# Latent attention with the values as the stationary operand, and softmax sums applied by channel

## What is computed

```python
q_nope, q_pe, k_nope, k_pe, v = ...      # per head: 64 + 32 query and key channels, 64 value channels
s = einsum('bqhd,bkhd->bhqk', q_nope, k_nope) + einsum('bqhr,bkr->bhqk', q_pe, k_pe)
p = softmax(s * scale, axis=-1)          # 256 queries, 512 keys (context and latent)
o = einsum('bhqk,bkhd->bqhd', p, v)
mix = o.reshape(b, 256, 1024) @ w_out
```

## Time and profile before

| | |
|---|---|
| median of three runs | 1434.42 us |
| the profiled execution, whole time | 1433.67 us |
| its span | 1431.8 us |
| TensorE busy | 1337.4 us (93%) |
| VectorE busy | 833.6 us (58%) |
| ScalarE busy | 558.0 us (39%) |
| mean granted clock | 0.976 |

### The profile page before, as it was taken

How to read it: one execution, slowest core, us unless ns; L and a number is a source line. 1 busy time by engine, 2 the same in 40 slices (tenths; PEclk the granted TensorE clock), 3 DMA queues, 4 the chain that set the end, 5 groups by cost and what they waited for, 6 DMA issues and landing times.

```text
span 1431.8 us, 16689 instructions
## 1 busy us (share of the span) xinstructions
PE 1337.4 (93%) x6768; PEld 1081.7 (76%) x6768; DVE 833.6 (58%) x1163; ACT 558.0 (39%) x739; POOL 3.5 (0%) x10
## 2 busy tenths in 40 slices
PE   5999879999899999999999999998789988799998
PEld 4877668888777778867777777887667766688887
DVE  5666666668664455563535352547556665667777
ACT  5354354455421122423131313125456553554542
POOL 0000000000000000000000000000000000000000
PEclk9999989999999999999999999999889998899999
DMA  8536365535554432454535353312021221235541
GB/s 306 196 118 250 121 275 211 196 130 206 198 180 181 198 118 88 164 218 147 206 141 212 136 217 137 140 51 92 30 83 48 96 81 60 110 137 207 193 176 59
DMA packets 23780, 218.75 MB, mean 153 GB/s; under 512 B 3104, under 2 KB 8224, under 8 KB 10656
## 3 DMA queue, kind: packets, MB, share of 16 engines
q1 hardware_dynamic: 21328, 209.67, 39.8%
q10 hardware_dynamic: 1520, 4.98, 0.9%
q0 software_dynamic: 864, 3.15, 0.6%
HBM read 216.74 MB, written 1.05 MB: 152 GB/s over the span
## 4 chain that ended last, share of the span: by engine, by line
PE 77%; DVE 12%; ACT 6%; issue 3%; DMA 1%; SPq 0%; DVEq 0%; ACTq 0%
PE bank L454 19%; PE bank L455 18%; PE bank L456 18%; PE bank L466 8%; PE bank L467 4%; DVE w_lo L1444 4%; PE mod_ps L503 3%; PE turned L482 3%; ACT w_hi L982 2%; DVE scaled L1485 2%; PE bank L867 2%; PE small L873 1%; DMA raw<-in_w_in 1%; DVE gated L1799 1%; PE small L522 1%
## 5 line engine op out<-in xcount | busy, mean ns | idle before, releaser
L1444 DVE TENSOR_TENSOR w_lo<-raw,w_hi 128x2048 fp32r<-128x2048 f32 (+4 forms) x168 | 338.2, 2054 | 80.4 <-ACT w_hi L982 79.8
L982 ACT ACTIVATE w_hi<-raw 128x2048 fp32r<-128x2048 f32 (+4 forms) x168 | 280.1, 1716 | 206.4 <-PE bank L456 169.6
L454 PE MATMUL bank<-act_parts,w_hi 128*128 128x512 f32 (+1 forms) x600 | 225.1, 375 | 1.8 <-DVE act_parts L1469 1.8
L466 PE MATMUL bank<-act_parts,w_hi 128*128 128x512 f32 x608 | 217.4, 402 | 6.6 <-DVE act_parts L1469 4.2
L455 PE MATMUL bank<-act_parts,w_hi 128*128 128x512 f32 (+1 forms) x600 | 221.8, 370 | 0.0
L456 PE MATMUL bank<-act_parts,w_lo 128*128 128x512 f32 (+1 forms) x600 | 221.6, 369 | 0.0
L467 PE MATMUL bank<-act_parts,w_lo 128*128 128x256 f32 x608 | 171.7, 282 | 0.0
L454 PE MATMUL bank<-w_hi,h_hi 128*128 128x512 f32 x392 | 154.5, 394 | 7.0 <-DVE h_lo L1721 3.6
L455 PE MATMUL bank<-w_lo,h_hi 128*128 128x512 f32 x392 | 152.8, 390 | 0.0
L456 PE MATMUL bank<-w_hi,h_lo 128*128 128x512 f32 x392 | 152.7, 389 | 0.0
L466 PEld LDWEIGHTS bank<-act_parts,w_hi 128*128 128x128 f32 x608 | 115.6, 190 | 35.3 <-DVE act_parts L1469 4.6
(11 more groups left out here) (234 smaller groups left out, 1636.9 us busy)
## 6 DMA issues: line engine op xcount, KB each, us to landing
raw<-in_ffn SPq DMA_DIRECT2D x35, 2048.0 KB, 7.7
raw<-in_mlp SPq DMA_DIRECT2D x24, 2048.0 KB, 7.6
raw<-in_mod_gate SPq DMA_DIRECT2D x7, 2048.0 KB, 7.7
raw<-in_conv_in SPq DMA_DIRECT2D x8, 1536.0 KB, 7.0
raw<-in_w_gates SPq DMA_DIRECT2D x4, 2048.0 KB, 8.3
raw<-in_w_branch SPq DMA_DIRECT2D x4, 2048.0 KB, 7.7
raw<-in_mla_q SPq DMA_DIRECT2D x4, 1152.0 KB, 5.1
raw<-in_w_in SPq DMA_DIRECT2D x2, 2048.0 KB, 14.2
```

The costliest lines, as they stand in the source:

```text
L454: te.matmul(dst, sh, mh, start=(j == 0), stop=False)
L466: te.matmul(b[:, :].rearrange("p (a t) -> p a t", a=2), sh, act_parts[:, :, 0, j, :], start=(j == 0), stop=False)
L982: act.activation(w_hi[:, s, part], raw[:, at % 2, part], ACT.Copy).then_inc(hi_ready, 1)
L1444: ve.tensor_tensor(w_lo[:, s, part], raw[:, at % 2, part], w_hi[:, s, part].bitcast(f32), ALU.subtract).then_inc(lo_ready, 1)
```

## The change

Values become stationary. For two heads of a token half (a pair) and each of the four key blocks, the 64 value columns of one head are loaded on the left half of TensorE's columns, those of the other on the right half, and the transposed probabilities stream past them. The result is transposed already: channels on the partitions, tokens along the row. prT has four buffers instead of two, and the values alternate between two buffers by group, so the vg copy goes. Pairs run after the scores in units 2, 4 and 6 and at the end of the group.

The reciprocal of a row sum must now be applied along the row. VectorE makes a diagonal matrix of the reciprocals (`sums_diag`), TensorE multiplies it by a matrix of ones (`spread_sums`), ScalarE copies the product to SBUF (`spread_copy`), and VectorE multiplies the values by it (`o_scaled`). ScalarE (`o_high`) and VectorE (`o_low`) then split the result for the projection, for a whole group at once during the next group; for the last group by token halves. The o_nat buffer, its four transpose calls and the splits behind them go. The projection (`o_rows`) reads o_hi and o_lo, and its first unit waits only for the first token half. On VectorE and ScalarE the split of the second projection chunk comes after the last of these steps. All four groups are written out; the loops go.

```diff
-            def mla_values(u, tr):
-                h = u % GH
+            def mla_values(g, pair, dst, tr):
+
+                t, p = pair // 2, pair % 2
                 te.wait_ge(tr_read, tr)
                 for j in range(4):
-                    last = te.matmul(small[:, u * VD:(u + 1) * VD], prT[:, u % 2, j, :], vg[:, j, h, :], start=(j == 0), stop=(j == 3))
+                    for e in range(2):
+                        last = te.matmul(dst[VD * e:VD * (e + 1), p * SEQ + t * P:p * SEQ + (t + 1) * P], v_of[g % 2][:, j, 2 * p + e, :],
+                                         prT[:, (2 * pair + e) % 4, j, :], start=(j == 0), stop=(j == 3))
                 last.then_inc(pv_done, 1)
+            def spread_sums(g, t, dst):
+
+                te.wait_ge(diag_ready, 2 * g + t + 1)
+                for p in range(2):
+                    for e in range(2):
+                        last = te.matmul(dst[VD * e:VD * (e + 1), p * SEQ + t * P:p * SEQ + (t + 1) * P], ones[:, :], diag[:, 2 * p + e, :],
+                                         start=True, stop=True)
+                last.then_inc(spread_done, 1)
...
-                    if u == 1:
-                        te.wait_ge(v_ready, n.step("v"))
-                    if u:
-                        mla_values(u - 1, trs[u - 1])
-                mla_values(7, trs[7])
+                    if u == 2:
+                        if g:
+                            te.wait_ge(o_ready, g)
+                        else:
+                            te.wait_ge(small_read, n.at("small"))
+                    if u in (2, 4, 6):
+                        mla_values(g, u // 2 - 1, values_of[u // 6], trs[u - 1])
+                    if u == 5:
+                        spread_sums(g, 0, sums_of[0])
+                spread_sums(g, 1, sums_of[1])
+                mla_values(g, 3, values_of[1], trs[7])
...
+            def o_rows(first=False):
+
+                s = chunk()
                 for t in range(NT):
-                    turn([o_nat[:, t, (4 * half + j) * P:(4 * half + j + 1) * P] for j in range(4)])
-            te.wait_ge(tr_read, n.at("tr"))
-            rotation(4)
-            rows_chunk()
-            rows_chunk()
+                    if first:
+                        te.wait_ge(o_lo_ready, MH // GH + t)
+                    b, q = unit(), slice(t * P, (t + 1) * P)
+                    product(b[:, :], [((o_hi[:, k, q], o_lo[:, (k + 2) % KT, q]), weights(s, k * COLS, (k + 1) * COLS)) for k in range(KT)],
+                            second=4 if t == 0 else None).then_inc(gemm_done, 1)
...
-                    if u == 0:
-                        act.wait_ge(pv_done, n.at("pv"))
-                        n.step("pv", 8)
-                        act.activation(vg[:, :, :, :].rearrange("p a h d -> p (a h d)"), v_next[:, :, :, :].rearrange("p a h d -> p (a h d)"),
-                                       ACT.Copy).then_inc(v_ready, 1)
-                        n.step("v")
+                    if g and u == 0:
+                        spread_copy(g, 2 * g, mod_ps, slice(0, SEQ))
+                    if g and u == 1:
+                        o_high(g, g - 1, slice(0, SEQ))
+                    if u == 6 and not following:
+                        spread_copy(g + 1, 2 * g + 1, mod_ps, slice(0, P))
...
+                else:
+                    o_high(g + 1, g, slice(0, P))
+                    spread_copy(g + 2, 2 * g + 2, bank[3], slice(P, SEQ))
+                    o_high(g + 2, g, slice(P, SEQ))
...
+            def sums_diag(g, t):
+
+                ve.wait_ge(probs_ready, 8 + 8 * g + 4 * t + 4)
+                rd = stat[:, RD + 4 * t:RD + 4 * t + 4]
+                chained(ve.reciprocal(rd, stat[:, LS + 4 * t:LS + 4 * t + 4]))
+                if 2 * g + t:
+                    ve.wait_ge(spread_done, 2 * g + t)
+                ve.tensor_tensor(diag[:, :, :], ident.rearrange("p (o n) -> p o n", o=1).to_broadcast([P, GH, P]),
+                                 rd.rearrange("p (h o) -> p h o", o=1).to_broadcast([P, GH, P]), ALU.mult).then_inc(diag_ready, 1)
...
                 for u in range(8):
+                    if u == 7:
+                        sums_diag(g, 1)
                     ve.wait_ge(tr_done, n.step("tr"))
-                    n.step("pv")
-                    if u >= 2:
-                        ve.wait_ge(pv_done, 8 + n.at("pv", 2))
-                    ve.tensor_copy(prT[:, u % 2, :, :], turned[(n.n["tr"] - 1) % 2][:, :].rearrange("p (a b) -> p a b", a=4)).then_inc(tr_read, 1)
+                    if u >= 4:
+                        ve.wait_ge(pv_done, 8 + 4 * g + u // 2 - 1)
+                    ve.tensor_copy(prT[:, u % 4, :, :], turned[(n.n["tr"] - 1) % 2][:, :].rearrange("p (a b) -> p a b", a=4)).then_inc(tr_read, 1)
                     if u + 2 < 8:
                         mla_max(u + 2)
+                    if g and u == 0:
+                        o_scaled(g, 4 * g, small, every)
+                    if g and u == 1:
+                        o_low(g, g - 1, every)
+                    if u == 4:
+                        sums_diag(g, 0)
```

## The result

| | median, us | lowest to highest | ratio to before (95%) |
|---|---|---|---|
| before | 1434.42 | 1432.33 to 1435.55 | |
| changed | 1426.47 | 1424.37 to 1428.52 | 0.9945 (0.993 to 0.996) |
| changed, a second set beside other runs of before (median 1434.23) | 1424.92 | 1424.56 to 1425.73 | 0.9931 (0.9915 to 0.9947) |

The change saves 8 to 9 us, 0.55% to 0.7%. The sign of the forecast holds; its 1430.5 lies 4 us too high. The first set lies 1 us inside the low end of its range (1425.5), the second 0.6 us outside. The profiled execution of the changed kernel takes 1428.52 us (span 1426.7), that of the second set 1425.73 (span 1423.9).

A forecast was written before the change was run, and what follows sets the result against it. TensorE carries 77% of the chain, with VectorE the bound at group ends and in the tail's hand-over. Groups + 4.2, last group and tail - 10.4, clock + 3.1 sum to - 3.1 from 1433.67: 1430.5 us, range 1425.5 to 1437.5.

The forecast's parts named there:

- The sign of the forecast: Whole kernel: faster, 1430.5 us against a median of 1434.42; faster by over 0.2% had chance 0.58.
- Value products: TensorE in latent attention: column halves run side by side, so a pair of heads takes 1.07 us, bounds 0.85 and 1.71.
- Rival 3: Value pairs: halves overlap only in part if loads can't run under a matmul; + 4.8, 1435.3 us, chance 0.13.
- rival 4: Value pairs: halves do not run side by side at all; + 10.1, 1440.6 us, chance 0.12.
- Spread sums: Two calls per group: 0.65 us each on TensorE, 0.95 us each on VectorE for reciprocal and diagonal product.
- A group with a following one: Groups 0 to 2: VectorE bounds the group's end and gets both diagonals; + 1.4 us each, + 4.2 in three groups.
- The saturated stretch: VectorE from copy 4 to the group's end, without pause: both diagonals add 1.9 us.
- The edits costed at nothing: Spread copy, o_hi, o_scaled and o_low in the next group's head periods 0 and 1: covered by projections in groups 1, 2.
- The wait ahead of the second spread: Group boundary: TensorE's idle time moves into one piece, estimated at 3.5 us, while VectorE finishes through the diagonal.
- Last group and tail: Group 3 to first projection chunk: first product 8.6 us earlier and full clock worth 1.8, together - 10.4 us.
- The clock: Group boundaries: the 3.5 us idle pieces bring half clock at all three; + 3.1 us, bounds - 1 and + 4.
- Rival 2: Group boundaries: the clock falls at no more of them than before; - 6, 1427.7 us, chance 0.20.

The follow-up runs named there:

- one_half: Changed kernel with value products issued head by head and both heads of a pair on the left column half; 1435.96 us, 1.0006 of the kernel before.
- head_by_head: Changed kernel with the two value-product loops swapped, one head's eight instructions before the other half's eight; 1432.71 us, 0.9987 of the kernel before.
- before_busy: Kernel before plus two unused score-sized products ahead of its last two value units in groups 0 to 2; 1433.51 us, ratio 0.9995.
- after_again: Changed kernel run once more without an edit, for a second trace; 1424.92 us, 0.9931 of the kernel before.
- tail_only: Kernel before with VectorE's w_lo of the next chunk moved behind the rows the projection needs; 1430.84 us, ratio 0.9975.
- late: Changed kernel with both diagonals of groups 0 to 2 moved behind normalise and their spread products into the next group; 1422.93 us, ratio 0.9919.
- late_busy: As late, with last-group o_hi one head and o_low two heads later, plus two unused score-sized products ahead of group 2's transpose 4; 1423.12 us.
- idle_longer: Changed kernel with the second diagonal product repeated three times ahead of itself on VectorE in groups 0 to 2; 1435.35 us, ratio 1.0000.

## Why the forecast came out as it did

**The number: in range in part by luck.** In the trace the stage and the first chunk became 9.75 us shorter, where - 3.1 was forecast, and 4.6 us were lost outside them, where nothing was forecast. The two errors have opposite signs. Without the second the profiled execution would have taken some 1424 us, below the range's 1425.5.

**Value products: right.** A pair was forecast at 1.07 us and takes 1.02; 16 instructions of 0.107 with the halves side by side are 0.85, the rest is entry, exit and slow start. The quarters of the earlier trace rows were the right row to go by. Rival 3, where loads can't run under a matmul, had 1.48. The Trainium skill (TensorE: Matmul & The Clock Gate, Part 3) says that weight loads overlap matmuls in flight only where the row group differs. The trace disagrees with it at 64 columns (1.02 us) as it did at 32. Rivals 3 and 4 fall. The price of rival 4 is of the right size (+ 10.1 forecast, 9.5 to 12.4 with one_half), though some of what was measured is the clock. head_by_head shows that its argument was not idle: the order of issue does matter, the overlap lives on the alternation.

**Spread sums: right, a little dear.** 0.60 each instead of 0.65, and 0.81 on VectorE instead of 0.95.

**A group with a following one: mechanism right, size 0.5 too large.** Copy 4 comes 0.59 earlier after the group's start (26.57 against 27.16; forecast 0.7). The saturated stretch grows by 1.35 (forecast 1.9: two diagonals are 1.62 and some small pauses went). The end behind copy 7 adds 0.14 (forecast 0.1 to 0.2). In group 0, at the same mean clock, the sum is + 0.90, not + 1.4; in group 1 the changed kernel's 37.64 at full clock stands against 36.68 of before_busy at full clock, + 1.0. With group 2 put at the same, three groups make + 2.8 instead of + 4.2. The edits costed at nothing in groups 1 and 2 do cost nothing there: VectorE still idles 4.17, 1.52 and 2.09 us around o_scaled in group 1. The wait ahead of the second spread, estimated at 3.5, is 2.8 to 3.0.

**Last group and tail: right, the sum in part by luck.** From transpose 0 to the first product 16.9 us were forecast; after_again takes 16.92 (1183.41 to 1200.33). The wait for exp 2 is 1.62 (1.9 forecast), that for the second diagonal 0.31 (0.7), and no other is noted: 1.9 us of waits instead of 2.95. TensorE is busy 15.0 us instead of the 14.0 forecast, and the two errors cancel. The first product follows the last pair at once, and the first chunk is 1.85 shorter (1.8 forecast). Of the tail's old cost, tail_only shows 3.0 to be the place of w_lo; the rest goes with the o_nat scalings, their transposes and splits, which no run takes apart.

**The clock: this step failed.** The forecast took + 3.1 because "an idle piece of 3.5 us is nearer to that than to the pieces under 1 us", that is, to the 3.91 in the tail, and so had all three boundaries fall. None fell, which the prediction had named as a sign that it is wrong. Windows of the changed kernel over the end of groups 0 and 2:

```profile
1095.00:1097.50 2.50, 1.18 (x18) 1.00 (x20) 2.43 (x6) 0.51 (x2) 0.00 (x0) 1.00 0.03 7
...
1172.50:1175.00 2.50, 0.06 (x2) 0.06 (x3) 2.47 (x5) 0.51 (x3) 0.00 (x0) 1.00 0.98 419
```

TensorE does next to nothing in the second of these 2.50 us and goes on at full clock. Rival 2 describes this, at 1427.7, and it is the case that came. With structure at + 2.8 for the groups, - 8.5 for the last group (24.41 in after_again against 34.09 is - 9.7, of which 1.1 is the half clock that the kernel before had on this group's transposes: 5.72 us up to the scores against 4.58) and - 1.85 for the first chunk, - 7.55 is explained of the 9.75. What is left, - 2.2, goes to the clock, where + 3.1 was forecast. It contains the falls of the kernel before at boundaries 2 and 3, now gone, less the new ones at 1163 and 1190. The analogy was wrong on both sides: in the tail the clock fell when TensorE had been idle for 0.65 us, and in tail_only with pieces of at most 1.41 us; and at the boundaries 2.8 to 3.0 us did not bring it down, 4.99 did. The trace of the kernel before could have told as much. It has a longer piece of idle time with full clock behind it, and a shorter one with half (each row is followed by the window behind its idle piece):

```profile
18.87 0.79 PE L454 MATMUL bank<-w_hi,act_parts 128*128 128x512 f32 x1 [3.86 <-DVE w_lo L1444]
...
18.87:21.37 2.50, 2.50 (x6) 2.02 (x7) 2.50 (x2) 0.00 (x0) 0.00 (x0) 1.00 0.96 390
...
148.97 1.30 PE L482 MATMUL turned<-tab,proj 128*128 128x128 f32 x5 [2.60 <-DVE act_parts L1500]
...
148.97:151.47 2.50, 1.94 (x8) 1.53 (x8) 1.14 (x2) 1.12 (x3) 0.00 (x0) 0.50 0.19 79
```

**The step that no term covered.** The stage with the first chunk is 9.75 us shorter in the trace, the profiled execution only 5.15. Of the 4.6 lost, 3.75 lie ahead of the stage, in code where the change leaves TensorE's work as it was: it issues 4949 matmuls up to the first kg transposes in both traces and gets there at 1058.77 instead of 1055.02. The other 0.85 lie behind the first chunk and were not taken apart. Windows from 360 to 365 us, first before, then changed; both kernels have just waited 2.07 us for the same VectorE row:

```profile
360.00:365.00 5.00, 5.00 (x23) 4.13 (x22) 4.86 (x3) 1.54 (x1) 0.00 (x0) 1.00 0.00 0
```

```profile
360.00:365.00 5.00, 5.00 (x17) 3.93 (x16) 4.43 (x3) 2.34 (x2) 0.00 (x0) 0.66 0.00 0
```

The one stays at full clock, the other doesn't and loses 1.6 us. The four traces of kernels with the old code ahead of the stage start it between 1053.95 and 1055.02 us, the ten with the new code between 1056.39 and 1060.50. The new kernel has one more VectorE instruction ahead of the stage and another layout of its code; which of these, or whether either, moves the falls of the clock was not tested and stays open. Counted from 1055.02, 1.4 to 5.5 us are lost there in every profiled execution of a kernel with the new code; what that part is in the executions behind the medians can't be read from them.

## What to carry to other kernels

Two products on disjoint column halves run side by side when their instructions alternate; write the loop so that neighbours in program order sit on different halves (1.02 against 1.52 us here). Work moved onto an engine that is saturated at a hand-over costs nearly its full time there (1.35 of 1.62 us in VectorE's stretch), even when the engine has pauses a few us later: look for those pauses first (late's median is 2 to 3.5 us lower by it, or 1 to 2.3 if each is counted against the kernel before in its own set). Read more than one idle piece before you reason from its length: the trace of the kernel before already held counterexamples. And when a step changes idle time of TensorE, carry the clock as a range of its own for each place, with both signs, instead of deciding it by the nearest idle piece; a fall that is mended in one place may come back in the next.

## What the runs showed of the hardware that was not expected

**The clock does not follow the length of one idle piece.** It stayed at full behind 2.83, 2.82 and 3.03 us at the boundaries of the changed kernel, and was at half behind 2.83 at the third of late and 2.82 at the third of late_busy. It was at half behind 1.81 in late, though not behind the 1.80 at that kernel's first boundary; 1.8 us after a wait of 1.62 it fell in one trace of the changed kernel and not in the other; and it was at half behind pieces of 0.98 and 1.41 in tail_only. At the first weight product of the program it was at full behind 3.86 us in one trace of the kernel before, at half behind 3.79 in the other. Behind 4.52 to 4.56 us (the start of group 0, in all 14 traces) and 4.99 to 5.20 (idle_longer) it was down each time. Within one kernel the falls mostly recur in the same places, so they are not plain chance; what decides them was not found, and two attempts to steer them (before_busy, late_busy) saved nothing.

**Overlap of column halves depends on the order of the instructions.** Eight instructions in a row on one half leave a part of the overlap, 1.52 us between 1.02 and 1.89. How far apart two instructions may stand was not measured.
